# A two-pass second half of the output projection, routing picked for two token tiles at a time, and the first expert's rows made by 0/1 products

## The reference, cut to what matters

```
x   = x + merged @ w_out                      # output projection, 1024 x 1024
h2  = rmsnorm(x, g_ffn)
lg  = h2 @ w_router_g + b_router_g            # 4 groups: take the largest
le  = h2 @ w_router_e + b_router_e            # 32 experts: top 2 of the 8 in that group
wts = softmax(lg)[group] * softmax(top2 values)
for each expert e: rows of h2 that chose e, in blocks
    y = (silu(xb @ w_gate[e]) * (xb @ w_up[e])) @ w_down[e] * w     # 1024 -> 256 -> 1024
x   = x + sum of the two experts' rows
x   = x + sigmoid(rmsnorm(x) @ w_ple_gate) * (p @ w_ple_proj);  out = rmsnorm(x)
```

## Time and profile before

| what | us |
|---|---|
| median of three runs | 933.08 (932.34 to 934.02) |
| the profiled execution | 934.07 |
| its span, first to last instruction | 931.9 |
| TensorE busy | 898.1 (96%) |
| VectorE / ScalarE / GpSimd busy | 504.0 / 343.2 / 195.8 |
| DMA traffic | 180.35 MB, mean 194 GB/s |

### The profile page before, as it was taken

The page is one execution under the profiler, slowest core; times in us unless marked ns, Lnnn a source line. Parts: engine busy times, 40 slices in busy tenths (PEclk is TensorE's granted clock), DMA queues, the critical chain, the costliest instruction groups (busy, mean ns, idle before and its releaser), DMA issues. The chain is left out here.

```text
span 931.9 us, 12362 instructions
## 1 busy us (share of the span) xinstructions
PE 898.1 (96%) x4864; PEld 661.8 (71%) x4864; DVE 504.0 (54%) x1043; ACT 343.2 (37%) x571; POOL 195.8 (21%) x169
## 2 busy tenths in 40 slices
PE   6999999999999999999999999999999999888896
PEld 5788788878877887888888888876555555444586
DVE  6378579759767999943333336375112112111766
ACT  5534453535355357622222243121122122112465
POOL 0052263327134433000000000002332332311000
PEclk9999999999999999999999999999999999999899
DMA  7520321122031111541222209959999999999701
GB/s 280 181 91 23 126 78 46 71 88 65 27 114 45 44 60 46 212 167 71 92 102 102 101 9 396 383 198 412 420 417 420 422 416 422 418 421 392 272 23 68
DMA packets 29233, 180.35 MB, mean 194 GB/s; under 512 B 5856, under 2 KB 6368, under 8 KB 18040
## 3 DMA queue, kind: packets, MB, share of 16 engines
q1 hardware_dynamic: 24056, 171.16, 46.8%
q0 software_dynamic: 5120, 8.41, 2.4%
HBM read 175.33 MB, written 12.59 MB: 202 GB/s over the span
## 5 line engine op out<-in xcount | busy, mean ns | idle before, releaser
L1108 PE MATMUL bank<-mT_parts,low_parts 128*128 128x512 f32 (+1 forms) x456 | 178.6, 394 | 0.0
L1108 PE MATMUL bank<-arena,cst 128*64 128x256 f32 (+2 forms) x918 | 133.5, 431 | 7.6 <-DMA arena<-in_w_expert 6.9
L1108 PE MATMUL bank<-mT_parts,x_parts 128*128 128x512 f32 (+1 forms) x328 | 132.7, 405 | 2.8 <-DVE arena L1783 2.3
L1108 PE MATMUL bank<-hT_parts,x_parts 128*128 128x512 f32 (+1 forms) x328 | 129.1, 394 | 0.0
L1718 DVE TENSOR_TENSOR low_parts<-arena,x_parts 128x1024 fp32r<-128x1024 f32 (+1 forms) x44 | 64.6, 1470 | 93.7 <-ACT x_parts L718 93.3
L2200 DVE TENSOR_TENSOR cst<-bank,chn 128x512 f32<-128x512 f32 x32 | 22.1, 692 | 164.8 <-PE bank L1518 164.8
L1108 PEld LDWEIGHTS bank<-arena,cst 128*64 128x64 f32 (+1 forms) x918 | 63.5, 138 | 61.6 <-issue 28.6
L1108 PEld LDWEIGHTS bank<-mT_parts,low_parts 128*128 128x128 f32 (+1 forms) x456 | 84.9, 186 | 21.5 <-DVE low_parts L1718 0.4
L1770 DVE SCALAR_TENSOR_TENSOR arena<-arena,chn 128x512 f32<-128x512 f32 x116 | 99.1, 912 | 0.0
L2351 POOL DMA_INDIRECT mT<-x_rows,table x32 | 33.1, 1034 | 270.5 <-DVE table L2130 257.8
L1108 PE MATMUL bank<-arena 128*128 128x64 f32 (+9 forms) x400 | 79.8, 332 | 0.0
(11 more groups left out here) (303 smaller groups left out, 1592.7 us busy)
## 6 DMA issues: line engine op xcount, KB each, us to landing
arena<-in_w_expert SPq DMA_DIRECT2D x19, 2048.0 KB, 28.8
arena<-in_w_expert SPq DMA_DIRECT2D x30, 1024.0 KB, 19.9
arena<-in_w_cm SPq DMA_DIRECT2D x32, 512.0 KB, 3.5
arena<-in_w_gate SPq DMA_DIRECT2D x7, 1536.0 KB, 6.7
hT<-in_w_expert SPq DMA_DIRECT2D x4, 2048.0 KB, 24.5
yT<-in_w_expert SPq DMA_DIRECT2D x4, 2048.0 KB, 27.5
arena<-in_w_tm SPq DMA_DIRECT2D x4, 1536.0 KB, 7.1
arena<-in_w_branch SPq DMA_DIRECT2D x8, 768.0 KB, 8.0
```

Of the source, the lines that this page charges most:

```text
L1108: return pe.matmul(out, lhsT, rhs, start=start, stop=stop)
```

## The change

Five edits, all between the projection and expert 0:

1. The second half of the projection runs in two passes. `low_first` (12 of the 24 products: `merged_low` x high for all k, and high x `wo_low` for k 4 to 7) is made for all four tiles first, then the other 12 of each. The turns and router products of tiles 4 to 6 move into the second pass, those of tile 7 behind it.
2. SyncE waits for the end of the first pass and then issues gate-and-up 4 (now whole) and down 3. Down 5 is issued only when the first expert's rows from tiles 0 and 1 are selected, down 6 when all are.
3. The gain g_ffn is multiplied into the router's weights once, earlier, on VectorE; the copies of the turned rows out of PSUM are then plain copies on ScalarE.
4. Roots and picks work on two tiles at a time; the first ranks' products move behind the projection.
5. (In VectorE's list `turned_block(0, 0, FIRST)` stands behind the entries of the rows' weights, L2154.) Expert 0's rows are not gathered and transposed: a 0/1 matrix `first_rows` (which row of each tile has which place in expert 0's block) is made by GpSimd for tiles 0 and 1 and by VectorE for tiles 2 and 3, and 32 products `x_sb` x `first_rows` give the block already transposed in a bank. The gathers start with expert 1. Most of the constant products go.

```diff
-        IN_HALVES = (4, 5) + tuple(n + RING for n in IN_HALVES_FROM)
+        IN_HALVES = (5,) + tuple(n + RING for n in IN_HALVES_FROM)
             up_weights(3)
+            sp.wait_ge(if_low_then_rows_selected, 2)
+            up_weights(4)
+            down_weights(3)
             for t in range(T - 1):
                 store_x2(t)
-                if t == 1:
-                    ...
-                    down_weights(5)
             sp.wait_ge(x2_mm, 2 * T)
             store_x2(T - 1)
-            down_weights(3)
             down_weights(4)
-            up_weights_in_halves(4)
             up_weights_in_halves(5)
             sp.wait_ge(x2_spilled, T * 16)
             ...
+            sp.wait_ge(if_low_then_rows_selected, 3)
+            down_weights(5)
+            sp.wait_ge(rows_turned, 1)
             down_weights(6)
@@ ScalarE
+            def turned_copy(i, first, end, bank, count):
+                act.wait_ge(x2_turned, count)
+                ...
+                act.activation(h2_piece[:, first:end, :], bank[...], ACT.Copy).then_inc(h2_ready, 1)
+            for i in range(2 * T - 1):
+                x2_square(i)
+                turned_copy(i, 0, 4, (S_16, OUT)[i % 2], i + 1)
+                if i >= T:
+                    x2_root(i)
+            x2_square(2 * T - 1)
+            turned_copy(2 * T - 1, 0, 2, OUT, 2 * T)
+            x2_root(2 * T - 1)
+            turned_copy(2 * T - 1, 2, 4, S_16, 2 * T + 1)
@@ TensorE
+            low_first = [(2, k) for k in range(KD)] + [(1, k) for k in range(KD // 2, KD)]
+            second_half = low_first + [(1, k) for k in range(KD // 2)] + [(0, k) for k in range(KD)]
+            for i in range(T + 1, 2 * T):
+                project(i, 0, LOW)
+            project(T, LOW)
+            project(T + 1, LOW, LOW + 5)
+            turn_half(T)
+            ...
+            project(T + 3, LOW + 5, LOW + 10)
+            pe.wait_ge(columns_then_logits_read, 2)
+            router(T + 2)
+            project(T + 3, LOW + 10)
+            constant_products(3)
+            turn_half(2 * T - 1)
+            pe.wait_ge(picked, 2)
+            mm(RANKS, const("upper"), tmp[:, 0:2, :], True, False)
+            mm(RANKS[:, NEXP:], ones, tmp[:, 0, :], False, True).then_inc(routing_mm, 1)
+            constant_products(2)
             router(2 * T - 1)
+            def select_first_rows(first, end):
+                for t in range(first, end):
+                    for k in range(KD // 2):
+                        for h in range(2):
+                            last = mm(FIRST[:, k * P + h * BLK:k * P + (h + 1) * BLK],
+                                      x_sb[:, t, h * 512 + k * P:h * 512 + (k + 1) * P], first_rows[:, t, :], ...)
             pe.wait_ge(slots_ready, 1)
             hits(0, 2, True, False)
-            constant_products(3)
+            pe.wait_ge(masked_then_first_rows, 8 * ROUNDS + 5)
+            select_first_rows(0, 2).then_inc(if_low_then_rows_selected, 1)
             pe.wait_ge(picked, T + 1)
+            mm(LAST_RANKS[:, NEXP:], ones, tmp[:, 2, :], False, False)
             mm(LAST_RANKS, const("upper"), tmp[:, 2:T, :], False, True).then_inc(routing_mm, 1)
-            constant_products(3)
 # totals, then hits(2, T)
+            pe.wait_ge(picked, T + 3)
+            select_first_rows(2, T).then_inc(rows_turned, 1)
             pe.wait_ge(slots_ready, 3)
             ...
-            constant_products(8)
-            turn_block(0, 0, rows_gathered[0], 16, first=True)
-            constant_products(4)
@@ VectorE
-            for t in range(T - 1):
-                h2_half(T + t)
-                row_root(t)
-                if t == T - 2:
-                    ranked(0, RANKS, 1)
-                pick(t, lambda: add_x2(T + t + 1))
+            add_x2(T + 1)
+            row_roots(0)
+            add_x2(T + 2)
+            pick(0, lambda: add_x2(T + 3))
-            h2_half(2 * T - 1)
-            row_root(T - 1)
-            pick(T - 1, lambda: None)
+            ranked(0, RANKS, 1)
+            row_roots(T - 2)
+            pick(T - 2, lambda: None)
             ranked(2, LAST_RANKS, 2)
+            chain(dve.tensor_tensor(first_terms, slot_rows[:, :, 2:T], oh[:, :, 2:T, 0:1]..., ALU.mult))
+            dve.tensor_tensor(first_rows[:, 2:T], first_terms[:, 0], first_terms[:, 1], ALU.add).then_inc(picked, 1)
             ...
+            turned_block(0, 0, FIRST)
@@ GpSimd
+            pool.wait_ge(slots_ready, 1)
+            for k in range(2):
+                for t in range(2):
+                    pool.tensor_scalar(first_terms[:, k, t, :], slot_of[:, k * T + t, :], oh[:, k, t, 0:1], None, ALU.mult)
+            pool.tensor_tensor(first_rows[:, 0:2], first_terms[:, 0], first_terms[:, 1], ALU.add)
-            for n in range(ROWS):
-                gather_rows(n, table[:, 0, n:n + 1], rows_gathered[n])
+            for n in range(1, ROWS + 1):
+                gather_rows(n % ROWS, table[:, 0, n:n + 1], rows_gathered[n % ROWS])
```

More of the change, by code:

```diff
@@ L982, in _, with x2_square @@
             wo_rounding(1, 0, KD)
-            for i in range(2 * T):
+            def x2_square(i):
                 t, total = i % T, (square_halves, ss2)[i // T]
@@ L1145, in gates @@
             def gates():
-                pe.wait_ge(w_if_split, 1)
+                pe.wait_ge(w_if_split_then_router_scaled, 1)
                 for k in range(KD):
@@ L1150, in gates @@
                                          k == 0, k == KD - 1)
-                last.then_inc(if_projected, 1)
+                last.then_inc(if_low_then_rows_selected, 1)
             def turn_columns():
@@ L1380, in project @@
                     pe.wait_ge(x2_ready, i - 3)
-                if i == T:
+                if i == T and first == 0:
                     pe.wait_ge(rounded, WO_REST_ROUNDED + KD)
-                for n, (part, k) in list(enumerate(last_tile_last if i == 0 else by_part))[first:end]:
+                order = second_half if i >= T else last_tile_last if i == 0 else by_part
+                for n, (part, k) in list(enumerate(order))[first:end]:
                     if i == 0 and part == 0:
@@ L1394, in project @@
                               n == 0, n == 3 * KD - 1)
+                if i == 2 * T - 1 and end == LOW:
+                    last.then_inc(if_low_then_rows_selected, 1)
                 if end == 3 * KD:
@@ L1496, in _ @@
             last.then_inc(routing_mm, 1)
-            for q in range(5):
-                mm(Y[0][:, :], ident, cst[:, 0:512])
+            pe.wait_ge(slots_ready, 2)
+            hits(2, T, False, True).then_inc(routing_mm, 1)
+            pe.wait_ge(picked, T + 3)
+            select_first_rows(2, T).then_inc(rows_turned, 1)
             pe.wait_ge(slots_ready, 3)
@@ L1509, in over_table, with turn_block @@
                 last.then_inc(routing_mm, 1)
-            def turn_block(n, slot, gathered, value, first=False):
+            def turn_block(n, slot, gathered, value):
                 pe.wait_ge(gathered, value)
-                if not first:
-                    pe.wait_ge(xT_ready, n)
+                pe.wait_ge(xT_ready, n)
                 for k in range(KD // 2):
@@ L2029, in add_x2, with row_roots @@
                     dve.tensor_tensor(part, part, (PA, PB, S_1, S_4)[i % 4][:, first:end], ALU.add).then_inc(x2_ready, 1)
-            def h2_half(i):
-                half = i // T
-                if i:
-                    dve.wait_ge(logits_done, i)
-                pieces = ((0, 4),) if i < 2 * T - 1 else ((0, 2), (2, 4))
-                for n, (first, end) in enumerate(pieces):
-                    dve.wait_ge(x2_turned, i + n + 1)
-                    dve.tensor_tensor(h2_piece[:, first:end, :],
-                                      (S_16, OUT)[(i + n) % 2][:, 0:(end - first) * P].rearrange("p (k s) -> p k s", k=end - first),
-                                      chn[:, G_FFN + 4 * half + first:G_FFN + 4 * half + end].unsqueeze(2).to_broadcast([P, end - first, P]),
-                                      ALU.mult).then_inc(h2_ready, 1)
-            def row_root(t):
-                rstd(rr2[:, t:t + 1], ss2[:, t:t + 1], offset=mean_halves[:, t:t + 1])
+            def row_roots(first):
+                pair = slice(first, first + 2)
+                root, total = rr2[:, pair], ss2[:, pair]
+                rooted_seen[0] += 2
+                dve.wait_ge(rooted, rooted_seen[0])
+                steps[0] += 1
+                dve.scalar_tensor_tensor(total, total, 1.0 / D, mean_halves[:, pair], ALU.mult, ALU.add).then_inc(dve_step, 1)
+                chain(dve.reciprocal(root, root))
+                chain(dve.tensor_tensor(total, total, root, ALU.mult))
+                chain(dve.tensor_tensor(total, total, root, ALU.mult))
+                chain(dve.tensor_scalar(total, total, -0.5, 1.5, ALU.mult, ALU.add))
+                chain(dve.tensor_tensor(root, root, total, ALU.mult))
             def spread(ap, shape, axis):
```

201 lines of the change are left out of this document (118 added, 83 removed).

## The result

| | before | after |
|---|---|---|
| median, us (15 runs each, beside each other) | 933.08 (930.96 to 934.48) | 937.29 (932.65 to 940.24) |
| ratio | | 1.0045 [1.0028, 1.0062] |
| profiled execution / its span, us | 934.07 / 931.9 | 937.29 / 935.3 |
| mean granted clock of it | 0.992 | 0.988 |

Slower by 0.45%, where 928.9 and faster were forecast. It is rival (c), nearly to the number, and by its mechanism: the granted clock fell. The stages first: engines' busy time, granted clock, DMA share, GB/s, to be held against the earlier trace rows.

What follows compares the result with a forecast made beforehand. The weight stream was taken to bound the end, TensorE's start counting only as it starts that stream. 1.0 us from expert 0's start and 3.3 from backlog, taken as 4.2, gave 929.9 profiled, 928.9 median; range 926.9 to 932.8.

Steps and rivals of the forecast that it cites:

- rival (c): Routing: clock falls near 626 to 1.2 GHz until expert 0, which starts about 645.5; time 938.0; chance 0.12.
- First pass, projection, picks: Second half of projection: first pass done at 604.8, projection ends 620.3, pick 2 starts 624.75, paired mask at 628.95.
- GpSimd's matrix: Before the selection: four 128x64 products at 0.5 us and a 128x128 sum at 0.9, 2.9 in all.
- The first expert's matrix: Routing: GpSimd's matrix, then TensorE's selection of tiles 0 and 1 from 626.6 to 629.95.
- Sixteen take 3.3: Selection on TensorE: 0.205 us per product, from the router products' row, so 3.3 us for sixteen.
- the start: Expert 0's start on TensorE: 637.95 instead of 638.97, 1.0 us earlier.
- VectorE's path: End of routing: table, entries and copy of expert 0's block end at 637.4, hiding the second selection.
- The stream: Expert weight loads: first refill issued at 639.95, lands at 644.1 against 648.4; stream and end about 4.2 earlier.
- the backlog gone: First refill: no earlier loads queued ahead, so it lands in 4.1 us instead of 7.4; 3.3 us gained.
- Rival (b): Weight stream: DMA idle time is moved, not filled; only TensorE's 1.0 us is gained; time 932.1; chance 0.10.
- The early loads: During the projection: gate-and-up 4 and down 3, 3 MB or 7.5 us of stream, move into idle DMA time.

Runs made afterwards that it cites:

- e1: After plus four 128-column constant products in TensorE's wait for GpSimd's matrix; 933.44 us, ratio to before 1.0007.
- e2: e1 plus one constant product before each pair of selection products (16 more); 933.45 us, ratio to before 1.0007.
- e6: e2 with a constant product before every second pair of selection products only (8, not 16); 931.51 us, ratio to before 0.9993.
- e9: e6 with the last ranks moved between tile 0's and tile 1's selection; 931.61 us, ratio to before 0.9989.
- e10: e9 with one constant product for each tile's selection (4, not 8); 936.24 us, ratio to before 1.0028.
- e3: After with expert 0 gathered and transposed again, its constants back, down 5 and 6 not awaiting selection, picks still paired; 937.17 us, ratio to before 1.0046.
- e11: e3 plus ten 128-column constant products in TensorE's wait for the paired mask; 932.99 us, ratio to before 1.0001.
- e4: Before without its constant products around the routing; 935.22 us, ratio to before 1.0027.
- e5: e2 with gate-and-up 4 and down 3 issued behind the projection again; 934.07 us, ratio to before 1.0012.
- e8: Before plus ten constant products (2.56 us) ahead of expert 0; 934.96 us, ratio to before 1.0034.

## Why the prediction was wrong, point by point

**First pass, projection, picks: right.** Loads of gate-and-up 4 and down 3 at 604.6 and 605.0 (604.8 foretold); the projection ends at 619.63 (620.3); pick 2 starts at 624.13 (624.75) and its mask is made from 628.07 to 628.29 (628.95). All a little early.

**GpSimd's matrix: right, over-priced.** 2.2 us by the first row, not 2.9: 0.42 for a 128x64 product, 0.45 for the 128x128 sum for which the earlier trace rows had 0.99.

**"The first expert's matrix": failed by the selection's price.** The sum took a clock of 1.00 through the routing for granted; the clock stood only in rival (c). "Sixteen take 3.3" came from the router's products in a row at a clock of 1.00. At that clock they took 3.78 as the row counts it (e1), 0.3 to 0.5 more than reckoned. In the changed kernel they took 6.78 and 7.09, ranks and totals 2.71 for the 1.48 of e1 and the weights' products 1.98 for 1.15. Rival (c) had every one of these: 6.6 each, expert 0 at 645.5 (644.48), time 938.0 (937.29). I gave it 0.12 because the longest wait I found was 1.1 us, and 622.5 to 641 before had 1.45 in all at a clock of 1.00. That comparison was the error: before, the constants, five of 512 columns among them, stood on both sides of the waits. The change took the most of them away, and what it added, selections without a gap, came with a clock of 0.50 for 18 us of busy TensorE. With constants among the selections the clock stayed at 1.00 (e2, e6, e9; e10's profiled execution), without them it fell (after, e1). e3 with e11 shows the same of constants in a wait, and e4 that the kernel before lived by its constants. What about the selections let the clock fall, their 64 columns, their fresh weights or something else, no run separates.

The Trainium skill, "TensorE: Matmul & The Clock Gate", section "HAM oscillation — how this bites in real kernels", tells of clock falls by long waits for DMA, which my sentence on it left out; its section "A second HAM failure mode: psum-queue depth-cycling" has a second kind, in a kernel that idles briefly and often between groups. This trace agrees in part with the second: the clock fell right behind an idle 1.06 us. What it has beyond that is a clock that stayed at 0.50 for 18 us without idle time.

**At full clock the start is as foretold, in part by luck.** e10's profiled execution and e6 are the change with its clock held: 637.72 and 638.23, and 637.95 was forecast. But they carry eight and twelve constants of 0.28 us that the forecast had not, e10 has its last ranks moved as well, and in e6 and e9 TensorE's order sets the start, not VectorE's path as reckoned (in e6 its copy of expert 0's block waits 0.56 us for TensorE). The mask's 0.7 us too early and the selections' higher price offset one another. No profile shows the change as built at a full clock. The parts: pairs with the gather cost 1.8 us at expert 0 (e11), and the selection in place of the gather gives 2.4 to 3.0 back (e9, e10 against e11).

**"The stream": failed, term 3.3 us ("the backlog gone").** Even e10's profiled execution wins 0.86 at g31, not 4.2. The table's fifth column is the reason: from the refill's issue to g31 it is 208.5 to 209.8 us in all thirteen, whether the queue was full when it was issued (before, e5), empty (e11) or in between. The refill itself did land sooner: in e11 it took 4.8 us, before 7.4. But the stream behind it moved fewer bytes. Here is e11 over 640 to 644, with the queue all but empty:

```profile
640.00:644.00 4.00, 4.00 (x37) 3.21 (x38) 0.60 (x1) 0.00 (x0) 1.00 (x1) 1.00 0.25 49
```

And here are the first 4 and 12 us from the refill's issue, and the rest up to g31, of before, after and e11:

```profile
640.95:644.95 4.00, 3.12 (x28) 2.18 (x26) 1.19 (x3) 1.65 (x2) 0.00 (x0) 1.00 1.03 414
640.95:652.95 12.00, 11.12 (x86) 6.41 (x84) 6.52 (x20) 3.26 (x6) 0.76 (x1) 1.00 1.01 411
652.95:850.36 197.41, 188.67 (x1355) 96.39 (x1353) 34.55 (x90) 38.64 (x88) 57.60 (x57) 0.99 1.01 420
```

```profile
647.31:651.31 4.00, 3.12 (x28) 2.02 (x26) 1.19 (x3) 1.65 (x2) 0.00 (x0) 1.00 0.77 250
647.31:659.31 12.00, 11.12 (x86) 6.25 (x84) 6.51 (x20) 3.26 (x6) 0.76 (x1) 1.00 0.92 331
659.31:856.51 197.20, 187.12 (x1355) 95.75 (x1353) 34.51 (x90) 38.65 (x87) 57.55 (x57) 1.00 1.01 419
```

```profile
642.73:646.73 4.00, 3.12 (x28) 2.18 (x26) 1.19 (x3) 1.65 (x2) 0.00 (x0) 1.00 0.75 256
642.73:654.73 12.00, 11.12 (x86) 6.41 (x84) 6.51 (x20) 3.26 (x6) 0.76 (x1) 1.00 0.90 330
654.73:851.20 196.47, 187.10 (x1355) 95.74 (x1353) 34.54 (x90) 38.64 (x87) 57.48 (x57) 1.00 1.01 419
```

In those 12 us before moved 4.93 MB, after 3.97 and e11 3.96. The 0.96 MB are 2.3 us at 411 GB/s: most of the 3.3 us won out of the backlog is lost again at once. Two thirds of it, 0.66 MB, are lost in the first 4 us, where the DMA engines have a share of 0.77 and 0.75: until the refill's bytes flow there is nothing to move (e11 moved 0.2 MB in its first 2 us), while before the backlog filled that time. My sum priced the landing of one transfer and left out this idle start of the stream. Why the rate stays lower from 4 to 12 us (372 and 367 GB/s, at a share of 1.00 and 0.98) is not explained by any run; from 12 us on the rates are equal (420 and 419). Of the last 1.0 us of the term e11 has 0.94 (208.47 for 209.41), after 0.21; the difference stays open. Rival (b), "only TensorE's 1.0 is passed on", was the right reading of this step to within a microsecond: the end moves with the refill's issue, which e8 shows on the kernel before. Its reason, down 5 and down 6 held back, is not the cause, for in e3 and e11 they are issued at about 624 and 625 and the term is missing as well.

The Trainium skill, "DMA: Bandwidth & Descriptors", section "Latency and other measured facts", has about 2 us of fixed cost. e11's refill of 1 MB, at 4.8 us with 2.5 of them bytes at 419 GB/s, has 2.3 at most; but the second half of the refill was under way too, and by all the bytes moved meanwhile (273 GB/s over 642.73 to 647.53, 1.31 MB, 3.1 us at 419) 1.7 are left. That doesn't tell the page's figure from my 1.6.

**The early loads** are worth some 0.5 us at most by what was measured (e5 against e2: 0.62 by medians, 0.5 by ratios, intervals overlapping): not told from nothing.

**Sum.** Forecast -4.2: -1.0 from the start and, rounded, -3.3 from the backlog. In the profiles the refill comes 6.36 us later instead of 1.0 earlier: 5.51 from expert 0's start and 0.85 because half of its up products took 2.83 and not 1.98. The backlog term gave 0.21, so g31 is 6.15 later. In time, by the ratios, e6 with its clock held stands 0.7 below before (not told from nothing) and after 4.9 above e6; that is the +4.2 measured.

## What to carry to other kernels

Before removing idle "constant" products, ask whether the clock holds once they are gone, even where TensorE is left without idle time: here it ran through 18 busy us at 0.50, and twelve products of 0.28 us put back were worth 4.9 us, where the change with its clock held is worth 1 or less (e6, e9). Look at the mean clock of every run, not at one profile: a kernel at the edge shows it as a wide spread (e10: 929 to 940). And when a stream of refills sets the end, time it from the first refill's issue; here moving bytes ahead of that point was worth 0 to 1 us of the 3.3 reckoned, and the end moved as much as the refill's issue, to within 1 us.

## What the runs showed of the hardware that I had not expected

- TensorE stayed at the 1.2 GHz level for 18 us in which the rows show it without idle time (626 to 644 us after), and came back during expert 0's products of 256 columns, within 644 to 648 (0.72, then 1.00). In e3 it came back during the 512-column constants: 0.50 over 634 to 636, 0.99 over 636 to 638.
- A selection product (fp32, 128x128 of weights, 64 columns) takes 0.23 us at a clock of 1.00 and 0.42 to 0.44 at 0.50: nearly all of it scales with the clock.
- The clock is not a property of the kernel alone: with four constants among the selections the same code had a mean clock of 0.997 or 0.998 in three executions and 0.985 to 0.995 in nine (e10). The profiled one, at 0.998, kept 1.00 through the routing.
- GpSimd's price of an elementwise operation is not set by its size alone: 0.45 us for a 128x128 addition here, 0.99 in the attention stage.
